# Second mixer: rotation partners copied by ScalarE, masks written by TensorE, exponentials read from PSUM, a new order of the heads

## The chip, the core and the metric

The kernel runs on one core of one Trainium2 chip. The metric is the device time of one execution in microseconds, the median of some runs; lower is better.

## The reference, cut to what matters

Two transformer-like blocks follow each other on 256 tokens of width 1024, all in float32: a feed-forward part, an RWKV-and-pooling mixer and a feed-forward part, then the second block: a mixer of two kinds of attention, a cross-attention on 256 memory rows, a squared-ReLU MLP and a norm. Only the second block's mixer is touched:

```python
h = rms_norm_2(x, g_mix)
qa, ka, va, qd, kd, vd = jnp.split(h @ w_in, splits, axis=-1)      # 512,128,128,512,512,512 columns
# rope: x1, x2 = split(x, 2);  concat([x1*c - x2*s, x2*c + x1*s]) on qa, ka, qd, kd, per head of 64
# sliding window ("swa"): 8 query heads, 2 key heads, blocks of 128, window 128, a sink per head
s = jnp.where(valid, q @ k.T * 0.125, -inf);  m = max(s.max(-1), sink)
e = exp(s - m);  p = e / (e.sum(-1) + exp(sink - m));  out_a = p @ v
# differential ("diff"): 4 heads, two maps each, causal
a = softmax(map 0) - lam * softmax(map 1);  od = a @ vd            # vd: 128 wide
out_b = rms_norm_2(od, g_diff) * (1 - lam_init)
x = x + concat([out_a, out_b]) @ w_out                             # rows 0..511: swa, 512..1023: diff
```

## The kernel before, in words

Products of weights are computed in fp32r (one pass of TensorE) with both operands split into a high and a low part. Weights arrive in 280 units of 128x1024 (512 KB each). For every unit ScalarE writes the high part into the ring `whi` (L1149, `split_hi`), VectorE the low part into `wlo` (L1652, `split_lo`); the rings hold six units (`RING`), the raw buffer three (`RAW`), and a helper `split_to(n)` on either engine catches up with the splits to unit n. The splits run some four units ahead of TensorE. Every engine runs its own list of instructions in program order, with semaphores between them; nothing is reordered, so the order written in the code is the schedule.

An input projection works on one unit of 128 output columns at a time. `a_unit` issues, for each of eight row chunks, a 512-column matmul (high weights against high and low activations side by side) and a 256-column one (low weights), so ScalarE has to copy half of the bank (`low`, L1261) and VectorE has to add it to the other half (L2142). `a_unit_summed`, which the first block's mixer uses, issues three 256-column matmuls for each chunk that all accumulate in one half bank. An output projection (`b_unit`, `b_last`) accumulates in banks PS0 to PS3, twelve 512-column matmuls for each unit; its eight units need `XT`, whose high part ScalarE and whose low part VectorE write (`rest`, L1696 and L1697).

The second mixer, `attention()`, has one part for each engine. Before it, the key/value projection of the cross-attention runs (16 units). The mixer's steps:

- Projection: 18 units (`N_WIN2`): 0 to 3 queries and 4 keys of swa, 5 values of swa, 6 to 9 queries, 10 to 13 keys, 14 to 17 values of diff. The banks are PS4, PS5, PS0, PS1. The rotation of the 13 query and key units: TensorE permutes the summed unit with the matrix `swap32` (fp32, all four passes) into a bank, VectorE multiplies by the cosine table (L2159) and the permuted one by the signed sine table (L2160) and adds (L2162). Values are turned by TensorE (L955) and copied by ScalarE (L1484). At the end TensorE makes `KSW`, the swa keys with their halves exchanged, by the matrix `swap64`, and VectorE copies it (L2165). Then both engines split two more units before the attention (`split_to(B_WOUT2 + RING)`).
- Attention: twelve jobs in the order `ORDER` (six of diff, then six of swa), each a full bank of 512 scores per row, in bank k % 4: with n = 1 two heads of 256 keys, with n = 0 four heads of 128 keys. `scores(k)` is TensorE's; heads use 64 rows of the array, the upper half for even heads and the lower for odd ones. `maxima(k)` on VectorE scales by 0.125, adds the mask and writes to SBUF (L2180, L2183, L2185, L2188), takes the maximum of each row (L2192, L2199) and for swa compares it with the sink (L2195, L2197). `exponents(k)` on ScalarE (L1500) takes the exponentials and their sums in place. `invert_sums(k)` on VectorE takes reciprocals (L2208 to L2215); GpSimd makes a diagonal matrix of them (`turner`, L2386, semaphore `p_ready`). `turn(k)`, nine of them, multiplies the probabilities by the diagonal, which transposes and normalises them at once; for diff it adds both maps. `turned(k)` on ScalarE copies the result to `PTS` (L1509).
- The products with the values (`pv_mm`), first those of diff, which are squared and summed (L1522), given a square root (L1529), inverted (L2223), normalised (L2226) and transposed back (L1043), while TensorE goes on with the turns and the products of swa. All eight units of the output projection come after both, rows 0 to 3 (swa) first.
- The norm transposes of the cross-attention (L561) start when the last unit has been added to `X`.

Of the kernel before, what the change touches and what calls it, by code (L numbers as in the profile page):

```python
# [14 lines left out]
P = 128  # L15
# [20 lines left out]
NEG = -1e30  # L36
# [83 lines left out]
def build(nc, t, out):  # L120

    ctx = ExitStack()
    with ctx:
# [138 lines left out]
        ODJ = ar(0, D)  # L262
# [14 lines left out]
        CLOW = ar(23552, 2, T)  # L277
        CTM = ar(24064, 2, T)
# [7 lines left out]
        def sems(names):  # L286
# [41 lines left out]
        rope_arg, rope_tab, lam_arg, lam_exp, q_low, q_sum, rope_mm, rope_done = \  # L328
            sems("rope_arg rope_tab lam_arg lam_exp q_low q_sum rope_mm rope_done")
# [4 lines left out]
        c_low, c_sum, ct_mm, ct_ev = \  # L334
            sems("c_low c_sum ct_mm ct_ev")
# [35 lines left out]
        W_BANKS, Q_BANKS, C_BANKS = (4, 5, 2, 3), (4, 5, 0, 1), (4, 5, 6, 7)  # L371

# [12 lines left out]
        def _(sp):  # L385
# [57 lines left out]
            for c in range(KC):  # L443
                load(B_WOUT2 + c, 0, rows("w_out_2")[:, c:c + 1, :])
# [25 lines left out]
        def _(pe):  # L470
# [438 lines left out]
            def attention():  # L909
# [30 lines left out]
                n_rope = n_vt = 0  # L940
                for i in range(N_WIN2 + 1):
                    if i < N_WIN2:
                        if i >= 4:
                            pe.wait_ge(q_sum, i - 3)
                        a_unit(B_WIN2 + i, 0, PS[Q_BANKS[i % 4]], None if i else "mix2")
                    k = i - 1
                    if k < 0:
                        continue
                    pe.wait_ge(q_sum, k + 1)

                    if k == 5 or k >= 14:
                        if n_vt >= 2:
                            pe.wait_ge(vt_ev, n_vt - 1)
                        for tt in range(NT):
                            last = pe.transpose(PS[7 - 4 * (n_vt % 2)][:, tt * P:(tt + 1) * P], QKV[:, k, tt * P:(tt + 1) * P], ident)  # L955
                        last.then_inc(vt_mm, 1)
                        n_vt += 1
                    else:
                        if n_rope >= 2:
                            pe.wait_ge(rope_done, n_rope - 1)  # L960
                        mm(PS[6 - 4 * (n_rope % 2)][:, 0:T], con("swap32"), QKV[:, k, :]).then_inc(rope_mm, 1)
                        n_rope += 1
# [21 lines left out]
                def turn(k):  # L984
# [5 lines left out]
                    if k >= 4:  # L990
                        pe.wait_ge(pt_ev, k - 3)
# [1424 lines left out]
```

## Time and profile before

| | |
|---|---|
| median of 3 runs | 994.62 us (994.14 to 995.46) |
| the profiled execution's own time | 995.92 us, span 994.0 us |
| busy share of the span | TensorE 96%, VectorE 67%, ScalarE 54%, GpSimd 3% |
| mixer's projection | 617.2 to 674.1 us of the span |
| mixer's attention | 674.1 to 715.0 us |
| mixer's output projection | 715.0 to 737.0 us |

In the rows, PE is TensorE's matmuls and PEld its weight loads, DVE is VectorE, ACT is ScalarE, POOL is GpSimd; L with a number is a line of the kernel. `128x512 f32` is partitions by elements. All matmuls made by the helper `mm` carry L472. An fp32 matmul shows as two records, each of two passes; one in fp32r shows as one. TensorE's matmuls are pipelined, so the time from one start to the next is their price, not their duration. PEclk is the granted clock as a share of 2.4 GHz.

### The profile page before, as it was taken

The numbers are of one execution on the slowest core, as the hardware profiler recorded it, in microseconds if no ns is written. First come the engines' busy times: TensorE is split into PE (matmuls) and PEld (weight loads), VectorE is DVE, ScalarE is ACT, GpSimd is POOL, SyncE is SP. The second block draws the span as 40 slices with busy tenths as digits, with TensorE's granted clock in tenths as the row PEclk, the third lists the DMA queues.
The fourth block names the chain that finished last, engine by engine and source line by source line (L and its number), as shares of the span: only waits on it lengthen the run. The fifth ranks groups of instructions, "written<-read, shape, count | busy, mean of one in ns | idle before, by whom it ended". The sixth has DMA issues, their size and how long they took to land.

```text
span 994.0 us, 17685 instructions
## 1 busy us (share of the span) xinstructions
PE 952.2 (96%) x6228; PEld 817.2 (82%) x6228; DVE 664.2 (67%) x1101; ACT 541.2 (54%) x980; POOL 30.0 (3%) x59
## 2 busy tenths in 40 slices
PE   6999999989989999999999999998899999999997
PEld 5788888879889877888888887887888888888885
DVE  4776766577786467766667785777457366666665
ACT  6564555477545337555555676546646446554452
POOL 3002000000000001000000000002100000000000
PEclk9999999999999999999999999997999999999999
DMA  7677766545220226766656665552047136665652
GB/s 216 201 220 216 207 186 189 154 128 149 85 66 4 65 87 168 212 186 185 189 185 195 189 182 157 170 169 86 1 117 222 49 123 191 191 201 177 194 186 85
DMA packets 204177, 153.62 MB, mean 155 GB/s; under 512 B 5323, under 2 KB 189872, under 8 KB 204128
## 3 DMA queue, kind: packets, MB, share of 16 engines
q1 hardware_dynamic: 202896, 151.08, 50.9%
q0 software_dynamic: 1232, 1.87, 0.9%
q8 instruction: 32, 0.52, 0.2%
q14 instruction: 17, 0.14, 0.0%
HBM read 151.89 MB, written 1.05 MB: 154 GB/s over the span
## 4 chain that ended last, share of the span: by engine, by line
PE 84%; DVE 7%; ACT 5%; issue 2%; DMA 2%; SPq 0%; DVEq 0%; ACTq 0%
PE ps L472 83%; DVE wlo L1652 2%; ACT whi L1149 1%; DMA raw<-in_w_ckv 1%; DMA raw<-in_ffn_w_gate 1%; DVE XT L1697 1%; ACT XT L1186 0%; DMA raw<-in_w_up 0%; ACT arena L1358 0%; DVE X L1720 0%; ACT arena L1170 0%; DVE arena L1889 0%; PE ps L561 0%; DVE arena L1844 0%; ACT arena L1351 0%
## 5 line engine op out<-in xcount | busy, mean ns | idle before, releaser
L472 PE MATMUL ps<-XT,whi 128*128 128x512 f32 (+1 forms) x1584 | 521.9, 382 | 7.5 <-DVE XT L1697 7.5
L1652 DVE TENSOR_TENSOR wlo<-raw,whi 128x1024 fp32r<-128x1024 f32 x280 | 337.1, 1222 | 107.6 <-ACT whi L1149 86.6
L472 PE MATMUL ps<-XT,wlo 128*128 128x256 f32 x1440 | 404.8, 281 | 0.0
L472 PEld LDWEIGHTS ps<-XT,whi 128*128 128x128 f32 x1584 | 289.9, 189 | 69.7 <-issue 7.6
L1149 ACT ACTIVATE whi<-raw 128x1024 fp32r<-128x1024 f32 x280 | 292.4, 1054 | 53.0 <-PE ps L472 21.1
L472 PEld LDWEIGHTS ps<-XT,wlo 128*128 128x128 f32 x1440 | 273.2, 190 | 3.2
L472 PE MATMUL ps<-whi,H 128*128 128x512 f32 x608 | 177.7, 393 | 2.8 <-issue 2.5
L472 PEld LDWEIGHTS ps<-whi,H 128*128 128x128 f32 x608 | 109.0, 188 | 26.0 <-issue 2.7
L472 PE MATMUL ps<-arena 64*64 64x64 f32 (+6 forms) x1576 | 99.6, 250 | 8.6 <-DVE arena L2185 2.0
L472 PEld LDWEIGHTS ps<-arena 64*64 64x64 f32 (+3 forms) x1576 | 91.1, 153 | 16.6 <-DVE arena L2185 2.9
L472 PE MATMUL ps<-wlo,H 128*128 128x512 f32 x304 | 95.6, 393 | 0.0
L472 PEld LDWEIGHTS ps<-wlo,H 128*128 128x128 f32 x304 | 57.1, 188 | 13.3
L472 PE MATMUL ps<-whi,XT 128*128 128x512 f32 x192 | 56.1, 400 | 0.3 <-DVE XT L1696 0.3
L1211 ACT ACTIVATE arena<-ps 128x256 f32<-128x256 f32 x44 | 16.7, 380 | 58.5 <-PE ps L472 58.5
L1221 ACT ACTIVATE arena<-ps 128x256 f32<-128x256 f32 x44 | 16.9, 384 | 48.8 <-PE ps L472 48.8
L472 PEld LDWEIGHTS ps<-whi,XT 128*128 128x128 f32 x192 | 35.4, 188 | 9.3 <-issue 1.6
L1229 ACT ACTIVATE H<-arena 128x256 fp32r<-128x256 f32 x44 | 18.4, 418 | 38.5 <-DVE arena L1797 38.5
L1261 ACT ACTIVATE arena<-ps 128x256 f32<-128x256 f32 x42 | 16.0, 380 | 41.5 <-PE ps L472 41.5
L1786 DVE TENSOR_TENSOR arena<-ps,arena 128x256 f32<-128x256 f32 x44 | 18.6, 423 | 28.0 <-ACT arena L1211 27.9
L1593 ACT ACTIVATE arena<-ps 128x256 f32<-128x256 f32 x32 | 12.2, 381 | 46.0 <-PE ps L472 46.0
L1800 DVE TENSOR_TENSOR H<-arena,H 128x256 fp32r<-128x256 f32 x44 | 18.7, 426 | 24.4 <-ACT H L1229 24.4
L1597 ACT ACTIVATE H<-arena 128x256 fp32r<-128x256 f32 x32 | 13.4, 418 | 35.4 <-DVE arena L2295 35.4
(255 smaller groups left out, 713.6 us busy)
## 6 DMA issues: line engine op xcount, KB each, us to landing
raw<-in_ffn_w_gate SPq DMA_DIRECT2D x44, 512.0 KB, 4.6
raw<-in_ffn_w_up SPq DMA_DIRECT2D x44, 512.0 KB, 3.9
raw<-in_ffn_w_down SPq DMA_DIRECT2D x44, 512.0 KB, 4.7
raw<-in_w_in SPq DMA_DIRECT2D x36, 512.0 KB, 3.9
raw<-in_w_up SPq DMA_DIRECT2D x32, 512.0 KB, 4.0
raw<-in_w_down SPq DMA_DIRECT2D x32, 512.0 KB, 4.6
raw<-in_w_out SPq DMA_DIRECT2D x16, 512.0 KB, 3.5
raw<-in_w_ckv SPq DMA_DIRECT2D x16, 512.0 KB, 4.6
```

The source lines that it names most:

```text
L472: return pe.matmul(o, st, mv, start=start, stop=stop, skip_group_check=True)
L1149: act.activation(whi[:, n % RING, :], raw[:, n % RAW, :], ACT.Copy).then_inc(hi_ready, 1)
L1211: act.activation(GL[:, q, :], PS[4 + q][:, T:2 * T], ACT.Copy).then_inc(g_low, 1)
L1221: act.activation(UL[:, q, :], PS[6 + q][:, T:2 * T], ACT.Copy).then_inc(u_low, 1)
L1229: act.activation(H[:, q, 0:T], HS[:, q, :], ACT.Copy).then_inc(h_hi, 1)
L1261: act.activation(dst[:, i % 2, :], bank[:, T:2 * T], ACT.Copy).then_inc(sem_low, 1)
L1593: act.activation(UL[:, q, :], PS[4 + q][:, T:2 * T], ACT.Copy).then_inc(r_low, 1)
L1597: act.activation(H[:, q, 0:T], HS[:, q, :], ACT.Copy).then_inc(r_hi, 1)
L1652: dve.tensor_tensor(wlo[:, n % RING, :], raw[:, n % RAW, :], whi[:, n % RING, :].bitcast(F32), sub).then_inc(lo_ready, 1)
L1697: return dve.scalar_tensor_tensor(XT[:, c, T:2 * T], ps, scale, hi, mul, sub)
L1786: dve.tensor_tensor(GS[:, q, :], PS[4 + q][:, 0:T], GL[:, q, :], add).then_inc(g_raw, 1)
L1800: dve.tensor_tensor(H[:, q, T:2 * T], HS[:, q, :], H[:, q, 0:T].bitcast(F32), sub).then_inc(h_ready, 1)
```

## The change

All of it is in the second mixer.

- Projection: units by `a_unit_summed`, in banks PS4 to PS7. ScalarE makes the rotation's partner by four copies of 32 partitions each from the bank (`SWP`); VectorE multiplies from the bank. The 13 `swap32` matmuls, the additions and the copies of the low halves are gone. Values are copied by VectorE. `KSW` is two ScalarE copies. `scores(0)`, `scores(1)`, their maxima and the exponentials of job 0 are placed between the last units. The splits of units 4 and 5 of the output weights come after `turned(8)` on ScalarE and after the diff rows' low parts on VectorE.
- Masks: three ScalarE copies in the attention's beginning put the unit matrix, zeros and the masks into `H` as fp32r; `scores(k)` begins with one matmul of 512 columns that writes the mask to the whole bank, and the scores accumulate on it. VectorE reduces from the bank; ScalarE's exponentials read the bank with scale 0.125. A bank is free for `scores(k + 4)` after the exponentials of job k. For n = 0 the sums are taken by VectorE from SBUF. `NEG` becomes -2^100.
- Order: scores and turns alternate; the products, square root, normalisation and transposes of the differential heads come before the last four swa turns; the output projection begins with the four units of the diff rows, of which three run among the turns 7 and 8 and ahead of swa's products with the values. The other five follow.

```diff
-NEG = -1e30
+NEG = -float(2 ** 100)
...
+        VALUES = (5, 14, 15, 16, 17)
+        OUT2_ROWS = (4, 5, 6, 7, 0, 1, 2, 3)
+        TURN_BANKS = (4, 5, 6, 5, 6, 7, 4, 7, 4)
...
-                        pe.wait_ge(sc_sum, k - 3)
+                        pe.wait_ge(sc_exp, k - 3)
...
+                    if n == 0:
+                        mask = bc(H[:, 0, 3 * P:4 * P], 4)
+                    elif kind == "swa":
+                        mask = bc(H[:, 0, 2 * P:4 * P], 2)
+                    else:
+                        mask = H[:, 0, P:4 * P].rearrange("p (a b k) -> p a b k", a=1, b=3)[:, :, 0::2, :].broadcast_to([P, 2, 2, P])
+                    mm(PS[k % 4][:, :], H[:, 0, 0:P], mask, stop=False)
...
+                        a_unit_summed(B_WIN2 + i, PS[C_BANKS[i % 4]], None if i else "mix2")
+                    if i - 1 in VALUES:
+                        k = i - 1
+                        pe.wait_ge(q_sum, k + 1)
...
+                    if i == 15:
+                        pe.wait_ge(rope_done, 13)
+                        scores(0)
+                    if i == 16:
+                        scores(1)
+                pe.wait_ge(vt_ev, 5)
+                pe.wait_ge(ksw_ready, 1)
...
+                    pe.wait_ge(yt_ready, N_MIXED + (4 if i < 4 else i + 1))
...
+                for k in range(2, 6):
                     scores(k)
+                turn(0)
+                scores(6)
+                scores(7)
+                turn(1)
+                scores(8)
+                scores(9)
+                turn(2)
...
+                scores(10)
+                scores(11)
+                turn(3)
+                turn(4)
+                for b in range(2):
+                    pe.wait_ge(pt_ev, 4 + b)
+                    for n in range(NT):
+                        pe.wait_ge(od_norm, n + 1)
+                        for h in (2 * b, 2 * b + 1):
...
+                turn(5)
+                turn(6)
+                pe.wait_ge(sc_exp, 12)
+                output(0, start=True)
+                turn(7)
+                output(1)
+                turn(8)
+                output(2)
...
+                act.activation(H[:, 0, 0:P], ident, ACT.Copy).then_inc(mask_set, 1)
+                act.activation(H[:, 0, P:2 * P], ident, ACT.Copy, scale=0.0).then_inc(mask_set, 1)
+                act.activation(H[:, 0, 2 * P:4 * P], CON[:, a:a + 2 * P], ACT.Copy).then_inc(mask_set, 1)
...
+                        sums = SUM[:, q:q + 1] if n else None
+                        ins = act.activation(e, PS[k % 4][:, m * nk:(m + 1) * nk], ACT.Exp, scale=0.125,
+                                             bias=NMX[:, q:q + 1], accum_out=sums)
...
+                            for a, b in ((0, 1), (1, 0), (2, 3), (3, 2)):
+                                ins = act.activation(SWP[QUADRANTS[a], n_rope % 2, :],
+                                                     PS[C_BANKS[i % 4]][QUADRANTS[b], 0:T], ACT.Copy)
+                            ins.then_inc(q_swap, 1)
...
+                        act.activation(KSW[TOP, :], QKV[BOTTOM, 4, :], ACT.Copy)
+                        act.activation(KSW[BOTTOM, :], QKV[TOP, 4, :], ACT.Copy).then_inc(ksw_ready, 1)
+                    if i == 17:
+                        exponents(0)
...
+                for k in range(1, 4):
                     exponents(k)
+                turned(0)
+                exponents(4)
+                exponents(5)
+                turned(1)
+                exponents(6)
+                exponents(7)
+                turned(2)
+                exponents(8)
...
+                for k in range(9, 12):
+                    exponents(k)
+                act.wait_ge(od_ss, 2)
+                act.activation(ODS, ODS, ACT.Sqrt, scale=1.0 / P, bias=con("eps_block")).then_inc(od_std, 1)
+                turned(3)
+                turned(4)
...
+                split_to(B_WOUT2 + RING)
...
+                    dve.tensor_reduce(NMX[:, q], PS[k % 4][:, :].rearrange("p (m k) -> p m k", m=m), AX_X,
+                                      mx).then_inc(own_dve, own.next())
...
+                    if n == 0:
+                        dve.tensor_reduce(SUM[:, q], SC[:, j, :].rearrange("p (m k) -> p m k", m=m), AX_X,
+                                          add).then_inc(own_dve, own.next())
+                        dve.wait_ge(own_dve, own.n)
...
+                        dve.tensor_copy(QKV[:, i, :], bank[:, 0:T]).then_inc(q_sum, 1)
...
+                        dve.tensor_tensor(RT[:, 0, :], bank[:, 0:T], RC, mul).then_inc(q_sum, 1)
+                        dve.tensor_tensor(RT[:, 1, :], SWP[:, n_rope % 2, :], RSN, mul).then_inc(own_dve, own.next())
+                        dve.wait_ge(q_sum, i + 1)
+                        dve.wait_ge(own_dve, own.n)
+                        dve.tensor_tensor(QKV[:, i, :], RT[:, 0, :], RT[:, 1, :], add).then_inc(rope_done, 1)
...
+                    if i >= 16:
+                        maxima(i - 16)
+
+                invert_sums(0)
+                for k in range(2, 12):
                     maxima(k)
-                    if k:
-                        invert_sums(k - 1)
+                    invert_sums(k - 1)
```

## Rows read from the trace of the kernel before

**Rows 1.** The page's chain that ended last, by engine (share of the span)

```profile
PE 84%; DVE 7%; ACT 5%; issue 2%; DMA 2%; SPq 0%; DVEq 0%; ACTq 0%
```

**Rows 2.** Windows (length, busy of PE, PEld, DVE, ACT, POOL, PEclk, DMA): most of the projection

```profile
639.50:674.00 34.50, 34.50 (x199) 30.25 (x197) 25.98 (x46) 16.10 (x28) 0.00 (x0) 1.00 0.53 167
```

**Rows 3.** Chain in order of time (start, us): projection begins, last two units, cross norm

```profile
617.22 22.11 PE ps L472 x122
...
668.26 2.78 PE ps L472 x16
671.26 2.80 PE ps L472 x16
...
737.04 0.67 PE ps L561 x6
```

**Rows 4.** Timeline of PE, `swap32` of one projection unit and of the next

```profile
655.02 0.60 PE L472 MATMUL ps<-arena,CON 128*128 128x256 f32 x2
...
658.24 0.59 PE L472 MATMUL ps<-arena,CON 128*128 128x256 f32 x2
```

**Rows 5.** Timeline of PE, first mixer, `a_unit_summed`: second and eighth chunk of one unit

```profile
224.36 0.40 PE L472 MATMUL ps<-XT,whi 128*128 128x256 f32 x2
...
226.51 0.40 PE L472 MATMUL ps<-XT,whi 128*128 128x256 f32 x2
```

**Rows 6.** Timeline of ACT and DVE within one projection unit

```profile
655.22 0.39 ACT L1261 ACTIVATE arena<-ps 128x256 f32<-128x256 f32 x1 [1.88 <-PE ps L472]
655.50 1.05 ACT L1149 ACTIVATE whi<-raw 128x1024 fp32r<-128x1024 f32 x1
...
655.98 0.41 DVE L2159 TENSOR_TENSOR arena<-arena 128x256 f32<-128x256 f32 x1
...
657.11 1.22 DVE L1652 TENSOR_TENSOR wlo<-raw,whi 128x1024 fp32r<-128x1024 f32 x1
```

**Rows 7.** Timeline of PE in the attention

```profile
676.37 2.10 PE L472 MATMUL ps<-arena 64*128 64x256 f32 x16 [0.52 <-DVE arena L2165]
...
688.13 3.78 PE L472 MATMUL ps<-LWG,arena 128*128 128x128 f32 x16
691.70 2.23 PE L472 MATMUL ps<-WPL,arena 128*128 128x128 f32 x16
...
710.33 3.11 PE L472 MATMUL ps<-arena 128*64 128x128 f32 x48 [0.69 <-ACT arena L1509]
```

**Rows 8.** Timeline of DVE: the mask of a swa job, written to SBUF

```profile
696.81 0.69 DVE L2180 SCALAR_TENSOR_TENSOR arena<-ps,CON 128x512 f32<-128x512 f32 x1 [2.14 <-PE ps L472]
```

**Rows 9.** Timeline of the cross-attention: maxima and exponentials that read the bank

```profile
766.80 0.68 DVE L2256 TENSOR_REDUCE arena<-ps 128x2 f32<-128x512 f32 x1
767.49 0.55 ACT L1564 ACTIVATE arena<-ps,arena,SMALL 128x256 f32<-128x256 f32 x1
```

**Rows 10.** Timeline: one square of eight, square root and normalisation of the differential heads

```profile
706.45 0.30 ACT L1522 ACTIVATE arena<-ps 128x128 f32<-128x128 f32 x1
...
710.30 1.28 ACT L1529 ACT_TABLE_LOAD   x1
711.59 0.30 ACT L1529 ACTIVATE arena<-arena,CON 128x8 f32<-128x8 f32 x1
...
712.16 1.29 DVE L2226 TENSOR_TENSOR arena<-ps,arena 128x512 f32<-128x512 f32 x2
```

**Rows 11.** Windows as in Rows 2: attention, around the two stretches of low clock

```profile
678.00:682.00 4.00, 2.03 (x16) 1.44 (x13) 3.93 (x9) 1.09 (x4) 0.00 (x0) 1.00 0.57 168
682.00:692.00 10.00, 10.00 (x37) 8.35 (x36) 9.55 (x26) 7.76 (x34) 4.53 (x6) 0.50 0.14 40
...
702.00:706.00 4.00, 4.00 (x23) 4.00 (x23) 1.08 (x7) 3.77 (x21) 2.08 (x2) 0.57 0.02 4
```

**Rows 12.** Timeline of POOL: the diagonal of an n = 0 job

```profile
688.83 1.04 POOL L2386 TENSOR_TENSOR arena<-CON,arena 128x512 f32<-128x512 f32 x1 [0.94 <-DVE arena L2215]
```

**Rows 13.** The page's DMA issues: output weights (us to landing)

```profile
raw<-in_w_out SPq DMA_DIRECT2D x16, 512.0 KB, 3.5
```

More of the change, by code:

```diff
@@ L277, in build @@
         CLOW = ar(23552, 2, T)
+        SWP = CLOW
         CTM = ar(24064, 2, T)
@@ L371, in build @@
         W_BANKS, Q_BANKS, C_BANKS = (4, 5, 2, 3), (4, 5, 0, 1), (4, 5, 6, 7)
+        VALUES = (5, 14, 15, 16, 17)
+        OUT2_ROWS = (4, 5, 6, 7, 0, 1, 2, 3)
+        TURN_BANKS = (4, 5, 6, 5, 6, 7, 4, 7, 4)
+        QUADRANTS = [slice(32 * k, 32 * k + 32) for k in range(4)]
         N_MIXED = NF + NT
@@ L442, in _ @@
                 load(B_WIN2 + i, 0, cols("w_in_2", i * P))
-            for c in range(KC):
-                load(B_WOUT2 + c, 0, rows("w_out_2")[:, c:c + 1, :])
+            for i, c in enumerate(OUT2_ROWS):
+                load(B_WOUT2 + i, 0, rows("w_out_2")[:, c:c + 1, :])
             for i in range(KC):
@@ L938, in attention @@
                 norm_t("mix2")
[L940 to L962, printed above, removed]
-                pe.wait_ge(rope_done, n_rope)
-                mm(PS[6][:, 0:T], con("swap64"), QKV[:, 4, :]).then_inc(rope_mm, 1)
-                pe.wait_ge(rope_done, n_rope + 1)
-                pe.wait_ge(vt_ev, 5)
                 def scores(k):
@@ L1003, in pt, with output @@
                     return PTS[:, g, i * P:(i + 1) * P]
-                for k in range(9):
-                    scores(k)
-                for k in range(3):
-                    turn(k)
-                for k in range(9, 12):
-                    scores(k)
-                for k in range(3, 5):
-                    turn(k)
-                pe.wait_ge(sc_sum, 12)
+                def output(i, start=False):
+                    c = OUT2_ROWS[i]
+                    pe.wait_ge(yt_ready, N_MIXED + (4 if i < 4 else i + 1))
+                    if i < KC - 1:
+                        b_unit(B_WOUT2 + i, 0, XT[:, c, :], start=start)
+                    else:
+                        b_last(B_WOUT2 + i, XT[:, c, :])
+                for k in range(2, 6):
+                    scores(k)
+                turn(0)
[5 more added lines that the diff above has]
+                turn(2)
                 pe.wait_ge(pt_ev, 3)
@@ L1037, in attention @@
                         last.then_inc(pv_mm, 1)
[L1038 to L1051 removed]
+                for i in range(3, KC):
+                    output(i)
             def cross():
@@ L1517, in attention @@
-                for k in range(3, 5):
-                    turned(k)
+                turned(0)
[6 more added lines that the diff above has]
+                exponents(8)
                 for n in range(NT):
```

221 lines of the change are left out of this document (99 added, 122 removed).

## The prediction

> **What bounds the kernel now.** I read the page's chain first: 84% of the span is TensorE [rows 1]. Then the windows of the part that is changed. In the projection TensorE is busy all the time at full clock, VectorE for 26 of 34.5 us, ScalarE for 16 [rows 2]: there only TensorE's own work counts. The chain gives the stage's ends: it starts at 617.22, its last matmul ends at 671.26 + 2.80 = 674.06, and the norm of the cross-attention starts at 737.04 [rows 3]. So the projection takes 56.84 us, and attention with output projection 62.98 us; the table above has the border between the two at 715.0, so 22.0 us are the eight output units and 41 us the attention. There TensorE is not the bound at first: the granted clock was 0.50 from 682 to 692 and 0.57 on average from 702 to 706, and ahead of the first of these the engine was busy for only 2.03 of 4 us while VectorE was busy for 3.93 [rows 11]. In that part VectorE writes each bank with its mask to SBUF (0.69 us) and then takes the maximum, and at 696.81 it had itself waited 2.14 us for TensorE [rows 8]: low clock and VectorE's passes push each other's work back.
>
> **Projection.** Below, t is the time after the end of its last unit. Before, a rotated unit comes every 3.22 us (655.02 to 658.24) [rows 4], a value unit every 3.00 [rows 3]. From the second to the eighth chunk of an `a_unit_summed` pass 226.51 - 224.36 = 2.15 us, so 2.15 / 6 = 0.358 us for a chunk and 2.87 for a unit [rows 5]. The copying engines: ScalarE's 256-column copy from a bank was followed by the next instruction 0.28 us after it began, so four take 1.12 to 1.6 us (0.28 to 0.39 each), and with the split of 1.05 us it is busy for 2.2 to 2.65 us of 2.87. VectorE needs 1.13 us for the three rotation steps (655.98 to 657.11) and 1.22 for the split, 2.35 in all [rows 6]. New waits: VectorE for `q_swap`, ScalarE for the unit's end; behind each the next split is queued, and TensorE waits for that one, but the splits are four units ahead. Both loads fit, so TensorE stays the bound: 18 x 2.87 = 51.6, three value transposes of 3.00 - 2.78 = 0.22 make 0.7, and `scores(0)` and `scores(1)`, which move in here, 2.2 (priced below). Sum 54.5 against 56.8: 2.3 us saved. The three mask copies run at the start of the key/value projection, four units ahead of need; I put them at nothing. If that cover were gone they would cost 1 us at most (three copies of about 0.3). The reordered loads are the same transfers of 512 KB on SP's queue.
>
> **Prices in the attention.** A record of a 128-column fp32 matmul: sixteen took 691.70 - 688.13 = 3.57 us, 0.223 each, in the half-clock stretch, so 0.112 at full clock [rows 7, 11]. A diff turn (16 records) is then 1.8 us, a swa turn 0.9, diff's products (24 records) 2.7, and swa's products took 3.1 [rows 7]. Scores: four jobs took 2.10 us [rows 7], about 0.53 each, because a job on the array's upper half runs beside one on the lower half. The mask is a 512-column fp32r matmul, not in the trace by itself; its nearest row is the unit of 2.78 us for 8 x (512 + 256) columns [rows 3], so 0.23. It uses all rows of the array, and stands between a job of the upper and a job of the lower half. Bounds: 0.23 + 0.53 = 0.76 if they still overlap, 0.23 + 0.90 = 1.13 if not (eight records at 0.112). I take 1.1. Maxima straight from the bank: 0.68 plus small steps, about 0.9 (1.05 with the sink); exponentials from a bank 0.55 each, so 1.1 a job, 1.3 with the sink's [rows 9], and four of 128 columns without a sum 0.30 each, by the square of 128 columns from a bank [rows 10] (up to 0.55 by rows 9), so 1.2. VectorE's pass of 0.69 [rows 8] for each of twelve jobs is gone (8 us), and returns for the four n = 0 jobs as a sum. The diagonal of an n = 0 job takes GpSimd 1.04 us [rows 12].
>
> **The new sequence.** TensorE: transposes of the last values at t = 0.5 (after VectorE's copy). ScalarE takes value 16, the exponentials of job 0 and value 17 in turn, 0.6 + 1.1 + 0.6 us, so `vt_ev` comes at 2.7; TensorE is idle for 2 us, as it is before the change. Scores 2 to 5 until 7.2; turn 0 until 9.0; scores 6, 7 until 11.2; turn 1 until 13.0; scores 8, 9 until 15.2. The exponentials of jobs 4 and 5 are queued behind `turned(0)` on ScalarE, so they run from 9.6 to 12.1, and job 5's sums, reciprocals and diagonal are ready at about 15.3, just in time for turn 2, which ends at 17.1. Its copy, 0.6; diff's products 17.7 to 20.4; scores 10, 11 until 22.7; turns 3, 4 until 24.5. Up to here TensorE sets the pace. Then it waits: the diff normalisation is queued behind the squares' second half (1.0 to 1.2, four of up to 0.30), three jobs of exponentials (1.3 + 1.4 + 1.4), a table load and the root (1.28 + 0.3), and VectorE's reciprocal and two products (0.2 + 1.29) [rows 10]: 20.4 + 8.2 = 28.6. So TensorE is idle from 24.5 to 28.6, where before swa's products stood. Transposes until 29.3, turns 5, 6 until 31.1. The diff rows' high and low parts are written meanwhile (last at about 31). Then nothing waits: eight units 22.0, turns 7, 8 1.8, swa's products 3.1, together 26.9. The splits of units 4 and 5, now behind `turned(8)` at about 39 and ready near 43, have output 2 and swa's products as cover (5.8 us); without it up to 2 us. With them SP's load of unit 7 moves back, to about 44; it lands 3.5 us later [rows 13], and the unit is used at about 55. End: 31.1 + 26.9 = 58.0, against 62.98: 5.0 us saved.
>
> **The clock.** At full clock the whole is 2.3 + 5.0 = 7.3 us. But TensorE's work is now what counts nearly throughout, and each microsecond at the lower level (1.2 GHz) costs up to 0.5 us. Ahead of the falls before the engine stood idle or worked on half of its rows. That comes twice again: idle 2 us then half-row scores (t = 1 to 7), and idle 4.1 us at t = 24.5. The second stretch before was about 3.4 us long (4 us at a mean of 0.57, so 4 x 0.43 / 0.5) [rows 11]. I take two such stretches, 7 us at the lower level, -3.5 us. Net: 3.8 us. On the profiled execution (995.92, its span 994.0 and 1.9 around it, which the change doesn't touch) 995.92 - 3.8 = 992.1; the median is 1.3 us lower than that execution, so 994.62 - 3.8 = 990.8.
>
> **A rule of the skill against a row.** The table load stood beside TensorE's work before, and is on the new chain: 1.28 us, and the root began 0.01 us after it [rows 10]. The Trainium skill (ScalarE: Activation LUTs, What ACT_TABLE_LOAD costs) puts a change of the function set at about 2.66 us, 1.28 of load and 1.38 of drain. By that the saving would be 1.4 us less, the time 992.2. The trace shows the load alone, with the engine's own queue empty behind it.
>
> **Rivals.** (1) Full clock nearly throughout: for it, the clock was 1.00 in the projection [rows 2], and the scores and turns are now denser; 994.62 - 7.3 = 987.3. (2) Nearly no gain: extra handovers in the alternating order. ScalarE serves turns and exponentials in one queue, so a late `turned` holds up exponentials and these hold up scores, since banks are freed by `sc_exp` and no longer by `sc_sum`. At 0.25 us of extra wait for each of twelve jobs 3 us go, 993.8. Against it: in my sequence the scores' banks are free 2 us ahead. (3) Slower, one mechanism: the clock falls at t = 1 to 5 and stays low, as for 10 us before [rows 11], and falls again at the wait of 24.5 and stays low through the first outputs. All of this is now on the path at 0.5 us for each microsecond; the gain of 7.3 is gone at 14.6 us of low clock, and 20 us give 997.3. Before, about 13.4 us were low (10 + 3.4), but TensorE was waiting for VectorE during half of it. Against it: scores and turns are now issued without pause from 2.7 to 17. (4) The change doesn't do what it says in the projection: ScalarE is the bound. It decides when a quadrant copy costs over 0.42 us ((2.87 - 1.05 - 0.1) / 4); at 0.55 each of 13 units takes 0.5 us longer, 6.5 us, time 997.3. The row's 0.39 speaks against it. (5) The table load on the new chain costs as much again as its row, 1.3 us, because the engine must run empty first: 992.1, inside the forecast's range, 0.05. [...]
>
> **How the numbers follow.** Forecast with one to three low stretches, 988.9 to 992.4: 0.47 (0.42 without (5)). Full clock, 985.5 to 988.9: 0.15. Little gain (2), 992.4 to 996: 0.24. Slower by (3), 996 to 999: 0.09. By (4): 0.05. The range 986.5 to 995.5 leaves out the last two, the upper edge of the little gain and the lower edge of full clock. Under 0.2% (2 us) a measurement of this kernel can hardly tell from no change. Faster than 992.6: 0.47 + 0.15 + a fifth of the little gain = 0.67; within: 0.21; slower than 996.6: 0.12.
>
> **What would show it.** Projection of 54.5 us with TensorE busy throughout and no wait for `SWP`. Maxima at about 0.9 us. `vt_ev` as the last wait before scores 2; the longest idle time of TensorE (about 4 us) ahead of the transposes that were L1043, with the root's chain as what ended it; PEclk low there. The output stage without a wait. Wrong, if TensorE waits for ScalarE's copies in the projection, if it waits for exponentials ahead of scores, or if PEclk is low for more than 10 us.

## The result and the profile after

The median is 1001.26 us (13 runs, 993.89 to 1005.74), against 995.67 us (13 runs, 994.14 to 998.8) for the kernel before on the same chip: ratio 1.0041, interval 1.0023 to 1.0059. The ratios and intervals, here and below, are estimated from fast runs alone, without the one run of k6_projmask that is over 1.5% above its fastest (1005.5 us), and are not quotients of medians, which here would be 1.0056. The change is slower, by a little, and above the range of the forecast. Of the 10.5 us between this median and the forecast of 990.8, 1.05 us are the starting point: the kernel before had a median of 994.62 in the three runs that the forecast stood on. The runs also lie further apart, 11.9 us against 4.7, and they follow the clock: each run lists its mean granted clock, and the two of the changed kernel at 0.996 took 993.89 and 994.49 us, the two at the lowest clock (0.984) 1004.13 and 1005.74 us.

The profiled execution took 996.73 us (span 994.9), against 995.92 before; it is one with little time at the lower clock. Its chain in order of time (start, us; the answers to [rows 3]):

```profile
617.27 20.52 PE ps L477 x168
...
673.08 0.23 PE ps L982 x2
...
675.44 17.60 PE ps L477 x96
...
736.36 0.67 PE ps L566 x6
```

The last matmuls of the projection, and the transposes behind them, on the timeline of PE:

```profile
672.79 0.28 PE L477 MATMUL ps<-XT,wlo 128*128 128x256 f32 x1
672.92 0.38 PE L982 MATMUL ps<-CON,arena 128*128 128x128 f32 x2
673.60 0.44 PE L982 MATMUL ps<-CON,arena 128*128 128x128 f32 x2 [0.30 <-DVE arena L2240]
```

The projection lasts from 617.27 to 672.92, 55.65 us; attention with output projection from there to 736.36, 63.44 us, against 62.98 before. The waits of PE between 620 and 735 us (us in total, times, longest):

```profile
PE ps L1056 <- ACT arena L1555: 3.1, 1, 3.1
PE ps L477 <- ACT arena L1541: 1.4, 1, 1.4
PE ps L477 <- ACT arena L1555: 0.7, 1, 0.7
PE ps L982 <- DVE arena L2240: 0.3, 1, 0.3
```

Four waits, 5.5 us, and all of them were in the sequence I had written down. What was not is the length of a job. The timeline of PE where scores 2 to 4 run (mask matmul, then the scores of the job):

```profile
675.44 0.50 PE L477 MATMUL ps<-H 128*128 128x512 f32 x1 [1.41 <-ACT arena L1541]
675.87 1.13 PE L477 MATMUL ps<-arena 64*128 64x256 f32 x4
676.93 0.50 PE L477 MATMUL ps<-H 128*128 128x512 f32 x1
```

From mask to mask 676.93 - 675.44 = 1.49 us: 0.43 from the mask to the first score and 1.06 for the scores. Here and below, a handover is a change of TensorE between matmuls on all 128 rows and matmuls on 64. At both handovers of a job the weight load is idle, and no semaphore accounts for it:

```profile
675.87 0.73 PEld L477 LDWEIGHTS ps<-arena 64*128 64x128 f32 x4 [0.25 <-issue]
676.92 0.19 PEld L477 LDWEIGHTS ps<-H 128*128 128x128 f32 x1 [0.33 <-issue]
```

It is the change of rows that costs, not the change of number format between fp32r and fp32: with all rows in use on both sides, the 16 fp32 records of turn 0 took 683.26 - 681.45 = 1.81 us up to the next mask, which is in fp32r, against 16 x 0.112 = 1.79, and the two fp32 records of `swap32` added 3.22 - 2.78 = 0.44 us to a unit in fp32r, against 4 x 0.112 = 0.45 [rows 3, 4]. From 64-row scores in fp32 to a full-row turn in fp32, where only the rows change, the extra is there: 681.45 - 680.36 = 1.09 us for 0.90.

Windows as in Rows 2, of the attention and the outputs (the answers to [rows 11]):

```profile
678.00:690.00 12.00, 12.00 (x70) 8.79 (x68) 7.73 (x22) 6.27 (x24) 3.92 (x5) 1.00 0.01 3
690.00:700.00 10.00, 9.31 (x67) 8.00 (x68) 4.70 (x18) 6.87 (x36) 2.33 (x4) 1.00 0.00 1
700.00:712.00 12.00, 8.78 (x51) 7.88 (x50) 5.67 (x16) 6.91 (x18) 2.19 (x3) 0.86 0.00 1
712.00:736.00 24.00, 24.00 (x149) 20.18 (x148) 11.23 (x14) 9.48 (x13) 0.00 (x0) 1.00 0.45 133
```

In this execution the attention had only one short stretch at the lower clock, behind the wait of 3.1 us: 12 x 0.14 / 0.5 = 3.4 us. The 0.9 us of span that it is longer than before are made of -1.2 in the projection, +0.5 in the attention and its outputs, and +1.6 behind them (994.9 - 736.36 = 258.54 against 994.0 - 737.04 = 256.96), where the cross-attention, which the change doesn't touch, had a stretch at the lower clock of 6 x 0.28 / 0.5 = 3.4 us that the profile of before has not (its clock was 1.00 from 740 to 850):

```profile
769.00:775.00 6.00, 3.97 (x23) 4.00 (x24) 2.37 (x8) 3.49 (x10) 0.00 (x0) 0.72 0.06 16
```

That the typical run is 4 to 5 us longer than this one was the question for the experiments.

### The profile page after: what moved, and what is told of

Same layout as the page of the kernel before. It is cut to its first block, busy times and chain, and to the rows that moved or that the text cites. A ratio compares the mean times of both kernels' runs of the same rounds, so it can differ in the third digit from the quotient of the medians.

```text
span 994.9 us, 17931 instructions
## 1 busy us (share of the span) xinstructions
PE 953.5 (96%) x6356; PEld 821.6 (83%) x6356; DVE 656.3 (66%) x1081; ACT 553.8 (56%) x1003; POOL 29.9 (3%) x59
## 3 DMA queue, kind: packets, MB, share of 16 engines
HBM read 151.89 MB, written 1.05 MB: 154 GB/s over the span
## 4 chain that ended last, share of the span: by engine, by line
PE 84%; DVE 7%; ACT 5%; issue 3%; DMA 1%; SPq 0%; DVEq 0%; ACTq 0%
PE ps L477 83%; DVE wlo L1706 2%; ACT whi L1177 1%; DMA raw<-in_ffn_w_gate 1%; DVE XT L1751 1%; PE ps L566 0%; ACT arena L1198 0%; ACT XT L1214 0%; DMA raw<-in_w_up 0%; ACT arena L1386 0%; DVE X L1725 0%; DVE X L1774 0%; DVE arena L1943 0%; DVE arena L2177 0%; DVE arena L1898 0%
## 5 line engine op out<-in xcount | busy, mean ns | idle before, releaser
L477 PEld LDWEIGHTS ps<-XT,whi 128*128 128x128 f32 x1728 | 307.7, 190 | 63.6 <-issue 7.8
L1177 ACT ACTIVATE whi<-raw 128x1024 fp32r<-128x1024 f32 x280 | 292.5, 1054 | 51.9 <-DMA raw<-in_ffn_w_gate 12.6
L477 PE MATMUL ps<-arena 64*64 64x64 f32 (+6 forms) x1576 | 102.3, 248 | 4.3 <-ACT arena L1372 1.7
L1239 ACT ACTIVATE arena<-ps 128x256 f32<-128x256 f32 x44 | 16.7, 380 | 56.4 <-PE ps L477 56.4
L1249 ACT ACTIVATE arena<-ps 128x256 f32<-128x256 f32 x44 | 16.7, 380 | 49.7 <-PE ps L477 49.7
L1647 ACT ACTIVATE arena<-ps 128x256 f32<-128x256 f32 x32 | 12.2, 382 | 44.8 <-PE ps L477 44.8
L1751 DVE SCALAR_TENSOR_TENSOR XT<-ps,VEC,XT 128x256 fp32r<-128x256 f32 x60 | 24.3, 475 | 10.6 <-ACT XT L1214 6.9
```

The source lines that it names most:

```text
L477: return pe.matmul(o, st, mv, start=start, stop=stop, skip_group_check=True)
L1177: act.activation(whi[:, n % RING, :], raw[:, n % RAW, :], ACT.Copy).then_inc(hi_ready, 1)
L1239: act.activation(GL[:, q, :], PS[4 + q][:, T:2 * T], ACT.Copy).then_inc(g_low, 1)
L1249: act.activation(UL[:, q, :], PS[6 + q][:, T:2 * T], ACT.Copy).then_inc(u_low, 1)
L1647: act.activation(UL[:, q, :], PS[4 + q][:, T:2 * T], ACT.Copy).then_inc(r_low, 1)
L1751: return dve.scalar_tensor_tensor(XT[:, c, T:2 * T], ps, scale, hi, mul, sub)
```

## The experiments

My theory, A: the masked jobs cost 0.39 us more each than I had put (12 x 0.39 = 4.7 us), and time at the lower clock falls on TensorE's own path. Rivals: the new order costs waits; the mask matmul itself is slow; the projection gained nothing. "Time at the lower clock" of a run is worked out below as (1 - mean granted clock) x span / 0.5.

**The two kernels again, unchanged.**

> The kernel before, unchanged, as its own partner, to have the granted clock of each of its runs beside its time. Theory A (the extra of the changed kernel is low clock that now lies on TensorE's path): this kernel's runs lie within about 5 us, and their times hang little on the clock (under 0.3 us for each us of low clock), since much of its low clock falls where TensorE waits for VectorE. Rival B (the changed kernel is slower by work that every run has, and the clock is noise for both): the same slope in both kernels, about 0.5.

> The changed kernel, unchanged. Theory A: runs from 994 to 1006 us again, on a line against the low-clock time (2 x (1 - mean clock) x span) with a slope of 0.4 to 0.6; at the clock of 0.996 about 994. Its profile shows low clock somewhere behind the score stage in runs over 1000 us. Rival B: spread of 2 to 3 us, no line.

Before: 996.16 us (ratio 0.9995, 0.9982 to 1.0008). After: 1000.40 us (1.0056, 1.0037 to 1.0075). The profiled execution of the second was a typical run, 1001.39 us. Its chain at the same place, its windows and its jobs on the timeline of PE:

```profile
671.52 0.23 PE ps L982 x2
...
740.58 0.67 PE ps L566 x6
```

```profile
674.00:678.00 4.00, 4.00 (x11) 1.97 (x11) 1.77 (x5) 1.76 (x8) 0.82 (x2) 0.80 0.01 2
678.00:683.00 5.00, 5.00 (x19) 4.11 (x19) 1.63 (x8) 1.02 (x4) 1.23 (x2) 0.50 0.01 3
683.00:690.00 7.00, 7.00 (x32) 5.62 (x33) 2.42 (x6) 2.67 (x9) 0.74 (x1) 0.74 0.00 1
...
706.00:715.00 9.00, 7.26 (x31) 6.67 (x32) 3.39 (x8) 4.46 (x10) 1.04 (x1) 0.62 0.01 2
```

```profile
677.28 0.80 PE L477 MATMUL ps<-H 128*128 128x512 f32 x1
678.00 2.07 PE L477 MATMUL ps<-arena 64*128 64x128 f32 x8
680.01 0.79 PE L477 MATMUL ps<-H 128*128 128x512 f32 x1
```

From the transposes to the cross norm 69.06 us, against 63.28 in the first profile. The clock fell after the idle time ahead of scores 2 and stayed at 1.2 GHz through the scores: (4 x 0.20 + 5 x 0.50 + 7 x 0.26) / 0.5 = 10.2 us; a job then takes 680.01 - 677.28 = 2.73 us. A second fall follows the wait ahead of the transposes, 9 x 0.38 / 0.5 = 6.8 us. The time differs between runs by this: over its 13 runs the changed kernel's time rises by 0.44 us for each microsecond at the lower clock, in this repeat by 0.43; the kernel before, over its 28 runs here, by 0.32, and in its own repeat by 0.23. (I had expected under 0.3 and a spread within 5 us for it; the 28 runs have 0.32 and 5.7.) Over all 68 runs of the kernel before on three chips it is 0.27, with a standard error of 0.03, and over the 22 of the changed kernel 0.44, with the same error. The amount is alike in both, a mean of 22.0 and 23.6 us against 22.5 and 23.7. So there is no more low clock than before over the whole kernel; each microsecond of it costs more.

**The new projection alone, and with the masks and the exponentials from the bank in the old order.**

```diff
# k5_proj: a_unit_summed, SWP, the value copies on VectorE, KSW on ScalarE; attention as before
-                        a_unit(B_WIN2 + i, 0, PS[Q_BANKS[i % 4]], None if i else "mix2")
+                        a_unit_summed(B_WIN2 + i, PS[C_BANKS[i % 4]], None if i else "mix2")
...
# k6_projmask: k5_proj, and
+                    mm(PS[k % 4][:, :], H[:, 0, 0:P], mask, stop=False)
...
+                        last = mm(PS[k % 4][:, m * nk:(m + 1) * nk], q, kt, start=False)
```

> The kernel before with the new projection alone (units by three 256-column matmuls, quadrant copies on ScalarE, values copied by VectorE); masks, exponentials and order as before. By the prediction: 56.8 - 51.6 - 0.7 = 4.5 us shorter projection, median 991.5. By the trace of the changed kernel, where scores 0 and 1 (2 x 1.49) lie in the 55.8 us: 52.8, so 4.0 us less, 992. Rival, ScalarE bound: 996 or more.

> The new projection, the masks by TensorE and the exponentials from the banks, but all jobs, turns and output rows in the order of the kernel before. If the masked scores' price (1.49 us a job against 0.53) is what ate the gain, this is slower than the one with the projection alone: 12 x 0.96 = 11.5 us more work on TensorE against about 9 us less on VectorE; I expect 992 to 996. Rival (the order ate it: TensorE's wait for the root's chain): this one keeps swa's products beside that chain and comes to 988 to 990.

The projection alone: 991.46 us, ratio 0.9953 (0.9935 to 0.9971), 4.6 us less than the 996.0 of the runs before. With the masks 1001.74 us, 1.0036 (1.0008 to 1.0064): 10.3 us are lost again, before any order is changed. The twelve runs fall into two groups, three of 990.61 to 992.74 us at a mean clock of 0.992 to 0.996, nine of 1001.07 to 1005.5 at 0.980 to 0.985, and I had expected 992 to 996, where none is. The profiled one (1005.5 us) is of the second group and the longest of the twelve, so its profile shows the far end of what this kernel does. The ten microseconds are not one price: this kernel also had more low clock than any other, a mean of 29.3 us against 22.1 for the projection alone. Windows of the attention, and the timeline of PE at the end of the long stretch:

```profile
674.00:677.00 3.00, 2.36 (x8) 1.49 (x9) 1.49 (x2) 2.42 (x4) 0.00 (x0) 1.00 0.45 164
677.00:701.00 24.00, 24.00 (x65) 15.63 (x64) 12.01 (x38) 9.72 (x40) 5.75 (x8) 0.50 0.15 45
701.00:705.00 4.00, 4.00 (x34) 3.76 (x33) 0.00 (x0) 1.47 (x3) 0.00 (x0) 1.00 0.00 0
```

```profile
695.04 2.07 PE L475 MATMUL ps<-arena 64*128 64x256 f32 x4
697.05 3.78 PE L475 MATMUL ps<-LWG,arena 128*128 128x128 f32 x16
700.62 2.15 PE L475 MATMUL ps<-WPL,arena 128*128 128x128 f32 x16
```

TensorE was busy for all of 24 us and at 1.2 GHz for all of them: it ran seven masked jobs of scores in a row, on one half of its rows at a time, and the clock came back only while the full-row turns ran, which began at 697.05. From this comes theory C: once the clock has fallen, it stays down while the engine works on half of its rows in turn with the masks.

By the medians the order would cost nothing, 1001.7 us with the old one and 1000.4 to 1001.3 with the new. But the two kernels differ in their low clock, and at a like clock they differ in time. The two runs of k6_projmask at 0.992 took 992.3 and 992.7 us; the three of the changed kernel at 0.992 took 996.6, 996.7 and 998.0. On a straight line through each kernel's runs, at 20 us of low clock, the kernel before takes 995.3 us, the projection alone 991.1, the masks in the old order 995.5, the changed kernel 999.5 (standard errors 0.2, 0.4, 0.5 and 0.2; for k6_projmask it is a place between its two groups; the kernel before is at 995.2, 995.0 and 995.5 on the three chips, so the chips don't make the difference). So the projection gains 4, the masks cost 4 and the new order another 4. "The order ate the gain" is not refuted: it is half of the answer. What in the order costs it is not isolated. TensorE waits 5.5 us in the new order's profile between 673 and 736 us, 3.1 of them for the root's chain, and 2.8 us in that of k6_projmask.

**Scores in pairs, so that the two halves of the array overlap again.** Two masks first, then the scores of two jobs in turn, one on the upper and one on the lower rows.

```diff
-                    mm(PS[k % 4][:, :], H[:, 0, 0:P], mask, stop=False)
...
+                    for x in (k, k + 1):
...
+                        mm(PS[x % 4][:, :], H[:, 0, 0:P], mask, stop=False)
+                    for a, b in zip(score_parts(k), score_parts(k + 1)):
+                        pass
...
-        ORDER = list(range(6, 12)) + list(range(6))
+        ORDER = list(range(6, 12)) + [0, 2, 1, 3, 4, 5]
```

> The changed kernel with the scores of two jobs issued as a pair: both masks first, then the scores of an upper-half and a lower-half job in turn; the swa jobs in the order 0, 2, 1, 3, 4, 5. My theory of the mis-sized term (1.49 us for each masked job in the trace where I had 1.1): it is lost overlap between the array's halves plus the exposed weight loads at each change between full and half rows. Then a pair takes about 1.9 to 2.2 us instead of 2.98, and the attention is 3 to 5 us shorter where TensorE sets the pace. Rival: the mask's matmul itself is slow (0.43 us for 512 columns); then a pair takes 2.8 us or more and the gain is under 1 us.

> New projection and masks by TensorE in the order of the kernel before (as the run that came to 1001.7 us with a low-clock stretch of 23.9 us at 677), but with the scores in pairs of an upper-half and a lower-half job. Theory C: the stretch lasted as long as scores on one half of the array's rows followed each other; with both halves at work it shrinks to 3 to 10 us, no run is over 996 us, median 986 to 990. Rival D (it starts with the idle time and the mask matmuls hold it, halves or not): still runs around 1000 us.

In the new order 992.68 us, 0.9966 (0.9954 to 0.9979), 7.7 less than the changed kernel's 1000.4 on that chip. In the old order 989.17 us, 0.9925 (0.9906 to 0.9943): 12.6 less than k6_projmask, and the fastest of all the versions with k11_oldorder_pair_fill below; none of the six runs of k9_oldorder_pair is over 991.6, as theory C had it. At a like clock (12 us of it) the gain by the pairs is 5.5 us in the new order (996.0 to 990.5) and 2.6 in the old (991.8 to 989.2); the rest is low clock that went with them, a mean of 16.6 us instead of 23.6 and 11.9 instead of 29.3. The intervals of k4_pair and k9_oldorder_pair don't meet: paired, the new order is the slower one by 3.5 us, of which 1.3 are left at a like clock, within the errors. And the fastest version is only 2.3 us below the projection with the old attention, with intervals that overlap (0.9906 to 0.9943 and 0.9935 to 0.9971): of the 5.0 us forecast for the attention little is there even when the jobs are paired. The timeline of PE in k4_pair:

```profile
674.52 0.73 PE L477 MATMUL ps<-H 128*128 128x512 f32 x2 [1.41 <-ACT arena L1542]
675.19 1.13 PE L477 MATMUL ps<-arena 64*128 64x256 f32 x8
676.25 0.73 PE L477 MATMUL ps<-H 128*128 128x512 f32 x2
```

Two jobs in 676.25 - 674.52 = 1.73 us where they took 2.98. Both masks together take 0.67, so the mask matmul is not slow by itself; that rival falls. The pair has two handovers where two single jobs have four: 0.67 is 2 x 0.23 and 0.21 more, and the 1.06 us for the scores of both jobs is what one took alone, so the two jobs overlap fully. Of the 1.25 us that a pair saves, about 0.9 are this overlap and 0.36 the two handovers. And the lower clock doesn't last. The windows of k9_oldorder_pair at the place where k6_projmask had its 24 us:

```profile
677.00:681.00 4.00, 2.93 (x18) 2.16 (x18) 2.41 (x10) 3.56 (x16) 1.84 (x3) 0.72 0.53 163
681.00:701.00 20.00, 17.66 (x142) 14.83 (x139) 13.72 (x43) 13.89 (x60) 7.24 (x9) 0.97 0.01 2
```

That is 24 x 0.5 / 0.5 = 24 us at the lower clock against (4 x 0.28 + 20 x 0.03) / 0.5 = 3.4 us, with the same masks, the same order of stages and more idle time of TensorE. It compares the longest run of one kernel with a middle one of the other, but the means over all runs (29.3 and 11.9) say the same.

**The masks left out.** The scores are computed without any mask, so this output is another function.

```diff
-                    mm(PS[k % 4][:, :], H[:, 0, 0:P], mask, stop=False)
...
-                        last = mm(PS[k % 4][:, m * nk:(m + 1) * nk], q, kt, start=False)
+                        last = mm(PS[k % 4][:, m * nk:(m + 1) * nk], q, kt)
```

> The changed kernel with its twelve mask matmuls left out (so the attention isn't masked), scores one job after another in its order. Theory C and the price: without the full-row matmul between them neighbouring jobs of different halves overlap again; two jobs in a row take 1.1 us instead of 2.98, and the median falls by 8 to 10 us, to 990 to 992, as with pairs or lower. Rival (the mask's own 0.22 us each is all): 12 x 0.22 = 2.6 us, 997.5.

992.92 us, 0.997 (0.9954 to 0.9986), 7.5 to 8.3 us less than the changed kernel (1000.4 and 1001.26), as much as by the pairs, though above the 990 to 992 that I had expected. Twelve masks at 0.23 would be 2.8 us. Without them the jobs join: scores 2 to 5, four jobs, stand as one row

```profile
675.54 2.57 PE L477 MATMUL ps<-arena 64*128 64x256 f32 x24 [1.41 <-ACT arena L1540]
```

of 2.57 us, where the changed kernel needed 681.45 - 675.44 = 6.01 for them. That is 0.64 us a job instead of 1.49. Of the 0.85 us, 0.23 are the mask's own, 0.36 the two handovers (0.20 + 0.16) and 0.26 the overlap of neighbouring jobs (0.90 - 0.64). The forecast had counted the first and the last; the handovers are what it lacked.

The Trainium skill (TensorE: Matmul & The Clock Gate, Part 3: Packing small matmuls) says that a weight load overlaps with running matmuls only when its row group differs. The idle 0.25 and 0.33 us of the weight load at the handovers agree, and so do the neighbouring jobs on different rows that overlap, here and in a pair. But a full-row weight load shares its rows with the full-row matmul ahead of it too, and there no handover price shows (the section names a background weight buffer as the other way to load ahead): in k3_fill below, nine full-row matmuls of 512 columns took 675.85 - 673.59 = 2.26 us up to the first score, 0.25 each with the handover in it. So the rule alone doesn't give the price.

**Work that only fills idle time, to keep the clock up.** Matmuls with the mask's operands into a free bank, at three places where TensorE waits: 8 ahead of scores 2, 12 ahead of the transposes, 10 in the cross-attention. In the kernel before: 7 ahead of its fifth job, 6 ahead of the differential heads' products, and the same 10; in k11_oldorder_pair_fill 8 ahead of the first job, 6 and 10; in k12_proj_fill 8, 7, 6 and 10.

```diff
+                for _ in range(8):
+                    mm(PS[7][:, :], H[:, 0, 0:P], H[:, 0, 0:512])
                 pe.wait_ge(vt_ev, 5)
...
+                pe.wait_ge(sc_exp, 9)
+                for _ in range(12):
+                    mm(PS[0][:, :], H[:, 0, 0:P], H[:, 0, 0:512])
...
```

> The changed kernel with idle time of TensorE filled: 8 full-array fp32r matmuls of 512 columns ahead of the wait for the last values, 12 ahead of the wait for the differential heads' transposes, 10 ahead of the cross-attention's turns, into banks that are free; they compute nothing that is used. Theory A: the granted clock stays at 1.0 in the mixer and the cross-attention, median 992 to 995, spread under 4 us. Rival B: no gain, or 1 to 2 us more where the fill outlasts the wait, 1000 to 1003.

> The kernel before with idle time filled in the same way: 7 matmuls ahead of scores 4, 6 ahead of the differential heads' products, 10 ahead of the cross-attention's turns. Theory A (low clock costs the kernel before less, as TensorE waits for VectorE there): low-clock time falls by 10 us or more and the median by 2 to 3 us, to 993 to 994. Rival (it costs 0.5 in both): 5 us or more, under 991.

> Paired scores and the filled idle times together. If both work on their own terms: paired 992.7, less 7 to 9 us of low clock at 0.4, 988.5 to 990. If the fill only delays, 993 to 994.

> The same as the paired scores in the old order, with the idle times of TensorE filled by matmuls that nothing uses. If low clock is still on the path there, 1.5 to 3 us less than without the fill and a spread under 3 us; if not, the same time.

> The new projection alone, old attention (991.5 us), with idle times filled. By the same step in the kernel before (2.5 us less) 989; if the low clock there is behind VectorE anyway, 990 to 991.

The changed kernel with fill: 995.05 us, 0.9989 (0.9974 to 1.0004), 5.3 us less than without, at 9.6 us of low clock instead of 23.6; median and spread (5.3 us) are a little above what A had said, and far from B. The kernel before with fill: 993.49 us, 0.998 (0.997 to 0.9991), 2.5 less, at 13.9 instead of 22.8. Over these, a microsecond of low clock taken away brought 5.3 / 14.0 = 0.38 us in the changed kernel and 2.5 / 8.9 = 0.28 in the one before: a difference of price the same way as between the runs of one kernel, now by an intervention. By the means of the runs it is 0.45 against 0.20; the intervals of the ratios are wide enough that the two prices nearly touch, so the lines through the runs are the better evidence. With pairs in the new order 990.74 us, 0.9948 (0.9932 to 0.9963), 2 us less than pairs alone, though above the 988.5 to 990 that I had expected; with the projection alone 990.12, 0.994 (0.9923 to 0.9956), 1.3 less, with overlapping intervals; with pairs in the old order 989.28, 0.9927 (0.9905 to 0.9948), nothing: its low clock was 11.5 us on average, with or without the fill (11.9).

## Why the prediction was wrong, point by point

- **The projection, right.** It took 55.65 us against a sum of 54.5. The two jobs of scores in it measured 1.47 us each instead of 1.1, so 0.74 of the difference is theirs; the 18 units and their transposes took 55.65 - 2.94 = 52.7 against 52.3. No wait of TensorE in it. ScalarE's four copies took 1.53 us (1.12 to 1.6), and in a window as in Rows 2 both copying engines keep slack:

```profile
649.79 1.53 ACT L1531 ACTIVATE arena<-ps 32x256 f32<-32x256 f32 x4
```

```profile
640.00:674.00 34.00, 33.70 (x266) 31.99 (x264) 24.54 (x41) 24.48 (x49) 0.00 (x0) 1.00 0.59 183
```

  k5_proj gained 4.6 us where this part of the sum says 56.84 - 52.3 = 4.5; rival (4) didn't come.
- **The price of a masked job, wrong: the first step that failed.** I took 1.1 us, between bounds of 0.76 and 1.13, for the case that mask and scores don't overlap. They took 1.49. The upper bound was a sum of two streams with their overlap lost, and left out the handovers: from the mask to the first score 0.43 instead of 0.23, and the eight passes of 64-row scores 1.06 instead of 0.90, with TensorE's weight load idle by 0.25 and 0.33 us at the two. Twelve times 0.39 is 4.7 us, near the whole gain that I had forecast for the attention (5.0). So the bound that I called upper was none. None of the rows that I had put down shows such a neighbourhood, but the trace of before does, in the same view from which Rows 5 are taken. In the first mixer four 64-row records of 256 columns stand ahead of a full-row matmul, at full clock:

```profile
222.44 1.10 PE L472 MATMUL ps<-arena,LWA 64*128 64x256 f32 x4 [0.89 <-ACT arena L1304]
223.47 0.70 PE L472 MATMUL ps<-arena,LWG 128*128 128x256 f32 x2
```

  They took 1.03 us, and 228.02 - 226.97 = 1.05 in the next unit, where the columns alone make 0.90; and the 256-column fp32r matmul ahead of the second group took 226.97 - 226.75 = 0.22 us instead of 0.11. Read from there, a masked job comes to about 0.34 + 1.05 = 1.4 us, and with ten such jobs the forecast gain of the attention goes from 5.0 to about 2 us.
- **The sequence, right in its waits.** Scores 2 began 2.5 us after the projection's last matmul (forecast 2.7), the wait ahead of the transposes was 3.13 us (4.1) and the longest; turn 0 began at 8.5 (7.2), and the transposes at 31.7 (28.6), later by 3.1, which is 10 x 0.39 for the jobs between, less the shorter wait of 1.0. Rival (2), extra waits between engines in the alternating order, didn't come: the 0.7 us that the products waited for `turned(2)` stood in the sequence with 0.6. What I hadn't asked is what the same jobs would take in the old order. The 4.1 us of wait were in my sum, and yet I took the new order for a gain; at a like clock it costs about 4 us with single jobs.
- **The prices from rows of like shape, right.** Sixteen records of a turn took 683.26 - 681.45 = 1.81 us (1.8), diff's 24 records of products 696.41 - 693.71 = 2.70 (2.7). The maxima's reduction from the bank took 0.69 us (0.68), an exponential from the bank 0.47 with the next 0.45 later (0.55), so ScalarE was a little quicker than forecast, off the path. The answers to [rows 8, 9]:

```profile
677.03 0.69 DVE L2202 TENSOR_REDUCE arena<-ps 128x2 f32<-128x512 f32 x1 [1.97 <-PE ps L477]
...
679.45 0.47 ACT L1514 ACTIVATE arena<-ps,arena 128x256 f32<-128x256 f32 x1 [0.47 <-DVE arena L2212]
```

- **The table load, right by the row.** On the chain it stands alone, and the root follows it at once:

```profile
701.89 1.28 ACT L1578 ACT_TABLE_LOAD   x1
...
703.19 0.30 ACT L1578 ACTIVATE arena<-arena,CON 128x8 f32<-128x8 f32 x1
```

  The 1.38 us of drain for each switch that the Trainium skill (ScalarE: Activation LUTs, What ACT_TABLE_LOAD costs) adds did not show; 0.02 us did. The measurement decides, and rival (5) is out.
- **The clock, wrong in its size: the second step.** The places were right: it fell after the idle time ahead of scores 2 and after the wait ahead of the transposes. I put 7 us at the lower level; the typical run had 10.2 + 6.8 = 17.0 us in this stage. Ten more at the 0.44 us of the line are 4.4 us; with the 4.7 of the jobs and the 1.05 of the starting point they make 10.2 of the 10.5 us by which the median missed the forecast. This is an account from one profile near the median, and no run measures the shares by themselves: k4_pair (7.7 us less) takes away more than the 0.39 of each job, and low clock as well, and k3_fill (5.3 us less) takes away low clock in the cross-attention too, about which the forecast said nothing. Both together gave 9.7.
- **Rival (3) came, with a chance of 0.09.** It had the mechanism (lower clock, on the path) and the decisive amount (14.6 us, against 17.0). The median is still above its 996 to 999, since the price of the jobs wasn't in it. The evidence that I held against it was that the engine works without pause from 2.7 to 17. The runs say that this isn't enough: the engine was busy without a break for 24 us in k6_projmask, and at 1.2 GHz all the while. I had written myself that the falls came where the engine "stood idle or worked on half of its rows", and then weighed only the idle time. That TensorE "was waiting for VectorE during half of" the low clock before is not in the rows either: it is busy for all of both stretches [rows 11]. That about half of each microsecond was hidden there is what the line through the 68 runs says (0.27 where 0.5 is the full price).

What stays open: why the clock stays down in some runs of a kernel and comes back early in others (the profiles of the changed kernel differ, 3.4 against 17.0 us in the stage), and whether half-row work or the masks between it is what holds it down. k10_no_mask, half-row work of both halves overlapping, had no fall there in its profile, which agrees with either; but neither had the first profile of the changed kernel, so one profile without a fall proves little. Open too is which part of the new order costs the 4 us.

## What to carry to other kernels

A matmul that uses all rows of TensorE between matmuls on 64 rows costs more than its columns: count the handovers, and what overlapped before and won't now; group such matmuls (all masks, then the scores of both halves in turn), which here turned 1001.7 us into 989.2 in the old order, 2.6 of it at a like clock and the rest by low clock that no longer came. Look for the price of a new neighbourhood in other stages of the same trace; here it stood in the first mixer. When a change moves the path onto TensorE, ask of every stretch in which its clock can fall what covered that time before; the same 22 us at 1.2 GHz cost 0.2 to 0.3 us each before, when waits for VectorE stood beside them, and 0.44 each afterwards. Compare versions at a like clock too: the medians of k6_projmask and of the changed kernel were alike, and hid an order that costs 4 us. And take the times of many runs with their clocks before a single profile is believed: the two of the changed kernel differ by 4.7 us.

## What the runs showed of the hardware

- The handover between a full-row fp32r matmul and 64-row fp32 matmuls cost about 0.2 us on each side (0.43 instead of 0.23; 1.06 instead of 0.90), at 2.4 GHz; between fp32 and fp32r on all rows no such price shows (1.81 us for 1.79); at 1.2 GHz a whole job took 2.73 us instead of 1.49.
- TensorE can be busy for 24 us in a row and stay at 1.2 GHz, when the work is 64-row scores alternating with masks; the clock came back while 128-row turns ran. With pairs of both halves the stretch at that place was 3.4 us.
- The time of the changed kernel varied nearly with the clock alone: over its 13 runs, time and low-clock time have a correlation of 0.98. In the kernel before it is 0.7 (28 runs).
